# A decoder layer's HGRN2 tail with two token buffers, evictions on ScalarE, and its transfers asked for earlier

## The reference, cut to what matters

```python
def gla_chunked(q, k, v, log_f, s0):
    ...
    def step(S, inp):
        qc, kc, vc, gc = inp
        bcum = jnp.cumsum(gc, axis=1)
        diff = bcum[:, :, None] - bcum[:, None, :]
        dec = jnp.exp(jnp.where(mask, diff, -jnp.inf))
        att = jnp.einsum('blhk,bshk,blshk->blsh', qc, kc, dec)
        o = (jnp.einsum('blsh,bshv->blhv', att, vc)
             + jnp.einsum('blhk,bhkv->blhv', qc * jnp.exp(bcum), S))
        b_last = bcum[:, -1:]
        S = (jnp.exp(b_last[:, 0])[..., None] * S
             + jnp.einsum('bshk,bshv->bhkv', kc * jnp.exp(b_last - bcum), vc))
        return S, o
```

## Time and profile before

| what | value |
|---|---|
| time, median of 3 runs | 1291.14 us (1289.27 to 1294.19) |
| the profiled execution's own time | 1291.79 us |
| its span | 1290.1 us |
| TensorE busy | 1186.7 us, 92% of the span |
| VectorE busy | 605.8 us, 47% |
| ScalarE busy | 445.0 us, 34% |
| mean granted TensorE clock | 0.945 |

### The profile page before, as it was taken

How to read it: one execution, slowest core, us unless ns; L and a number is a source line. 1 busy time by engine, 2 the same in 40 slices (tenths; PEclk the granted TensorE clock), 3 DMA queues, 4 the chain that set the end, 5 groups by cost and what they waited for, 6 DMA issues and landing times.

```text
span 1290.1 us, 25363 instructions
## 1 busy us (share of the span) xinstructions
PE 1186.7 (92%) x10272; PEld 1024.3 (79%) x10272; DVE 605.8 (47%) x1082; ACT 445.0 (34%) x789; POOL 441.2 (34%) x370
## 2 busy tenths in 40 slices
PE   5999999988977769998898899998999999999998
PEld 5999987855654449887797865997999999987775
DVE  4699645236386568512437245257433433421003
ACT  6333243255543123432445134354322322321212
POOL 6443531153406202254251400242344344333331
PEclk9999999989958769898898999998999999999999
DMA  5332321075628730334240676131232322322221
GB/s 143 83 97 67 99 71 52 5 214 179 206 75 276 218 117 4 99 115 117 91 139 20 194 229 196 49 99 44 83 88 86 90 87 86 93 84 82 82 82 69
DMA packets 176381, 139.02 MB, mean 108 GB/s; under 512 B 16007, under 2 KB 162872, under 8 KB 176266
## 3 DMA queue, kind: packets, MB, share of 16 engines
q1 hardware_dynamic: 166610, 115.98, 30.4%
q0 software_dynamic: 7200, 20.23, 5.0%
q10 hardware_dynamic: 2456, 1.21, 0.3%
HBM read 129.41 MB, written 7.97 MB: 106 GB/s over the span
## 4 chain that ended last, share of the span: by engine, by line
PE 71%; DVE 15%; ACT 4%; DMA 3%; issue 3%; POOLq 2%; POOL 2%; SPq 0%; DVEq 0%; ACTq 0%
PE PS L262 64%; PE PS L265 7%; DVE PROJ L1908 3%; DVE SC L681 2%; POOLq L462 2%; DMA W_scratch<-in_cache_moba_v 2%; DVE PROJ L1909 1%; DVE XN L909 1%; DVE XT L681 1%; POOL W_LO L246 1%; DVE PROJ L681 1%; DVE XN_parts L901 1%; DVE XN L681 1%; DMA PROJ<-in_x_sample 1%; ACT W_HI L237 0%
## 5 line engine op out<-in xcount | busy, mean ns | idle before, releaser
L246 POOL TENSOR_TENSOR W_LO<-W,W_HI 128x1024 fp32r<-128x1024 f32 x128 | 314.9, 2465 | 649.3 <-ACT W_HI L237 649.3
L262 PE MATMUL PS<-XN_parts,W_HI 128*128 128x272 f32 x1184 | 340.6, 288 | 0.0
L262 PE MATMUL PS<-OM_parts,W_HI 128*128 128x272 f32 x960 | 277.6, 289 | 0.0
L262 PEld LDWEIGHTS PS<-XN_parts,W_HI 128*128 128x128 f32 x1184 | 223.2, 188 | 0.0
L237 ACT ACTIVATE W_HI<-W 128x1024 fp32r<-128x1024 f32 x128 | 134.2, 1053 | 210.3 <-PE PS L262 210.3
L262 PE MATMUL PS<-OM_parts,W_LO 128*128 128x272 f32 x704 | 203.9, 290 | 0.0
L262 PE MATMUL PS<-SC_parts,W_HI 128*128 128x272 f32 x608 | 180.0, 296 | 4.3 <-POOL W_LO L246 3.1
L262 PEld LDWEIGHTS PS<-OM_parts,W_HI 128*128 128x128 f32 x960 | 181.9, 189 | 0.1
L262 PE MATMUL PS<-SC_parts,W_LO 128*128 128x272 f32 x608 | 176.9, 291 | 0.0
L262 PEld LDWEIGHTS PS<-OM_parts,W_LO 128*128 128x128 f32 x704 | 132.3, 188 | 0.0
L262 PEld LDWEIGHTS PS<-SC_parts,W_HI 128*128 128x128 f32 x608 | 115.7, 190 | 8.4 <-issue 6.3
(11 more groups left out here) (394 smaller groups left out, 2109.7 us busy)
## 6 DMA issues: line engine op xcount, KB each, us to landing
W<-in_w_gu SPq DMA_DIRECT2D x44, 512.0 KB, 3.8
W<-in_w_in SPq DMA_DIRECT2D x30, 512.0 KB, 3.8
W<-in_w_down SPq DMA_DIRECT2D x22, 512.0 KB, 3.7
W_scratch<-in_cache_moba_k SPq DMA_DIRECT2D x64, 128.0 KB, 2.4
W_scratch<-in_cache_moba_k POOLq DMA_DIRECT2D x64, 128.0 KB, 2.5
W_scratch<-in_cache_moba_v SPq DMA_DIRECT2D x64, 128.0 KB, 3.3
W_scratch<-in_cache_moba_v POOLq DMA_DIRECT2D x64, 128.0 KB, 3.5
W<-in_w_xkv SPq DMA_DIRECT2D x16, 512.0 KB, 3.7
```

What stands on the lines that cost most here:

```text
L246: nc.gpsimd.tensor_tensor(hi_lo(n)[1], raw_chunk(n), hi_lo(n)[0].bitcast(F32), ALU.subtract).then_inc(S("weights_split"), 1)
L262: return nc.tensor.matmul(out, lhsT, rhs, start=start, stop=stop, skip_group_check=True)
```

## The change

- HGRN2 gets a tail of its own (`hgrn_tail_tensor`, `hgrn_vector_tail`, `hgrn_tail_scalar`). Token-order keys and values have two buffers for the prompt and one for the samples, token PSUM banks 0 and 1 alternate, outputs use banks 3 and 6, state products 4 and 5. The order of tiles is 0, 1, samples, 2, 3.
- ScalarE makes the token copies (one of 128x512 per tile) and the output copies. The masked values are made by VectorE (4 samples) and ScalarE (4).
- SP asks for the states, decay tiles 0 and 1 and the two rows of log decays between quarters 42 and 44; decay tiles 2, 3 and 4 after its last quarter and level 7. Tiles 0 and 1 are made ready during levels 4 and 5, tiles 2 to 4 in the tail; GDN's first steps no longer make tiles 2 and 3.
- The 17 transposes of the probabilities stand ahead of level 0; each level is then followed by the four quarters that followed the next level before. All 32 value quarters stand ahead of the tail's first transposes.
- GDN's tail is the old code, alone.

```diff
+        def g_decay(i):
+            return g_dec[:, i] if i < 4 else g_dec_s[0:NS]
...
+        h_kv = carve(XN, 1760, 512), carve(XN, 2272, 512), carve(SC, 1120, 512)
...
-            load_pages(sp, [n for n in range(NPG, 64) if issuer(n) == "sync"])
-            after(sp, "ssm")
+            load_pages(sp, [n for n in range(NPG, 44) if issuer(n) == "sync"])
             sp.wait_ge(S("ssm_states_out"), 32)
             sp.dma_start(t_s0, a["state_hgrn"][0].rearrange("b (c e) k v -> (e k) b c v", e=2)).then_inc(S("state_in"), 16)
-            def spread_decays(tile, dst, w, landed="g_spread"):
-                src = decay_rows[:, tile * P:tile * P + w].rearrange("(o h) l -> o h l", o=1)
-                sp.dma_start(dst, src.to_broadcast((w, H, w))).then_inc(S(landed), 16)
+            def spread_decays(i, landed):
+                t0, w, _ = TILES[i]
+                src = decay_rows[:, t0:t0 + w].rearrange("(o h) l -> o h l", o=1)
+                sp.dma_start(g_decay(i), src.to_broadcast((w, H, w))).then_inc(S(landed), 16)
             sp.wait_ge(S("decay_rows_out"), 16)
-            sp.wait_ge(S("h_lv_mm"), H_MM[7])
-            spread_decays(0, g_dec[:, 2], P)
-            spread_decays(1, g_dec[:, 3], P)
-            spread_decays(4, g_dec_s[0:NS], NS)
+            spread_decays(0, "g_spread")
+            spread_decays(1, "g_spread")
             for e in range(2):
                 sp.dma_start(g_logd[e * DH:(e + 1) * DH, :, :],
                              decay_rows.rearrange("(o c e) t -> e o c t", o=1, e=2)[e].to_broadcast((DH, 2, T))).then_inc(S("g_spread"), 16)
+            load_pages(sp, [n for n in range(44, 64) if issuer(n) == "sync"])
+            sp.wait_ge(S("h_lv_mm"), H_MM[7])
+            for i in range(2, NT):
+                spread_decays(i, "g_spread_late")
             after(sp, "hgrn")
-            spread_decays(2, g_dec[:, 0], P, "g_spread2")
-            spread_decays(3, g_dec[:, 1], P, "g_spread3")
...
-        h_vm_ = carve(SC, 2 * T, NB * H * DH)
+        h_vm = carve(PROJ, (C_Z + 4) * T, H, NB, DH)
...
+                if j in (4, 5):
+                    decay_vector(v, j - 4)
...
+        H_TURNS = (0, 1, 4, 2, 3)
+        H_AT = {i: x for x, i in enumerate(H_TURNS)}
+        def h_kv_of(i):
+            return h_kv[i % 2] if i < 4 else h_kv[2][0:NS]
+        def h_turned(i):
+            return bank(H_AT[i] % 2)
+        def h_added(i):
+            return bank(4 + i % 2)[:, 0:2 * DH]
+        def h_out(i):
+            w = TILES[i][1]
+            return bank((3, 6)[H_AT[i] % 2])[:, 0:2 * w]
+        def hgrn_tail_tensor(pe):
+            def turn(i):
+                t0, w, _ = TILES[i]
+                x = H_AT[i]
+                if x >= 2:
+                    pe.wait_ge(S("tail_tok_out"), x - 1)
+                for m_, src in enumerate((h_kd, h_v)):
+                    for k in range(2):
+                        last = tr(h_turned(i)[0:w, 256 * m_ + k * P:256 * m_ + (k + 1) * P], src[:, k, t0:t0 + w], P)
+                last.then_inc(S("tail_tok"), 1)
+            def added(i):
+                kv = h_kv_of(i)
+                pe.wait_ge(S("tail_tok_out"), H_AT[i] + 1)
+                if i >= 2:
+                    pe.wait_ge(S("tail_state"), i - 1)
+                for h in range(H):
+                    last = mm(h_added(i)[h_rows[h], (h // 2) * DH:(h // 2 + 1) * DH], kv[:, h * 64:(h + 1) * 64],
+                              kv[:, 256 + h * 64:256 + (h + 1) * 64], True, True)
+                last.then_inc(S("tail_st"), 1)
+            def output(i):
+                t0, w, _ = TILES[i]
+                kv = h_kv_of(i)
+                if H_AT[i] >= 2:
+                    pe.wait_ge(S("h_o_out"), H_AT[i] - 1)
+                o_ = [h_out(i)[h_rows[h], (h // 2) * w:(h // 2 + 1) * w] for h in range(H)]
+                for h in range(H):
+                    last = mm(o_[h], kv[:, 256 + h * 64:256 + (h + 1) * 64], h_att_of(i, w, h), h < 2, i == 0)
+                if i == 4:
+                    pe.wait_ge(S("state_in"), 32)
+                    for b in range(NB):
+                        own = slice(b * TS, (b + 1) * TS)
+                        for h in range(H):
+                            last = mm(o_[h][:, own], t_s0[h_rows[h], b, h // 2, :],
+                                      h_qe[h_rows[h], h // 2, t0 + b * TS:t0 + (b + 1) * TS], False, True)
+                elif i:
+                    pe.wait_ge(S("tail_state"), i)
+                    for h in range(H):
+                        last = mm(o_[h], t_st[i % 2][h_rows[h], h // 2, :], h_qe[h_rows[h], h // 2, t0:t0 + w], False, True)
+                last.then_inc(S("tail_o"), 1)
+            pe.wait_ge(S("tail_prep"), 1)
+            turn(0)
+            turn(1)
+            yield
+            pe.wait_ge(S("g_beta"), UNITS + 2)
+            added(0)
+            output(0)
+            turn(4)
+            added(1)
+            turn(2)
+            output(1)
+            pe.wait_ge(S("tail_tok_out"), H_AT[4] + 1)
+            output(4)
+            turn(3)
+            yield
+            added(2)
+            output(2)
+            pe.wait_ge(S("tail_vm"), 2)
+            pe.wait_ge(S("tail_root"), 2)
+            for h in range(H):
+                last = mm(bank((2, 7)[h // 2])[h_rows[h], :], h_kv[2][0:NS, h * 64:(h + 1) * 64],
+                          h_vm[0:NS, h].rearrange("p b d -> p (b d)"), True, True)
+            last.then_inc(S("tail_st"), 1)
+            added(3)
+            output(3)
+            yield
+        def h_vm_part(b):
+            return h_vm[0:NS, :, b, :], h_kv[2][0:NS, 256:512].rearrange("p (h d) -> p h d", d=DH), ind[0:NS, b:b + 1]
+            tt(h_kd, hk, h_d, ALU.mult).then_inc(S("tail_prep"), 1)
+            yield
+            def state(i):
+                old, new = t_st[i % 2], t_st[(i + 1) % 2]
+                if i >= 2:
+                    v.wait_ge(S("tail_o"), H_AT[i - 1] + 1)
+                if i:
+                    link(tt(new, old, bc(t_lastp[:, i, :].rearrange("p (c o) -> p c o", o=1), (P, 2, DH)), ALU.mult))
+                v.wait_ge(S("tail_st"), (1, 2, 3, 5)[i])
+                add = h_added(i).rearrange("p (c d) -> p c d", d=DH)
+                last = tt(new, new, add, ALU.add) if i else V.tensor_copy(new, add)
+                last.then_inc(S("tail_state"), 1)
+                v.wait_ge(S("tail_state"), i + 1)
+            state(0)
+            decay_vector(v, 2)
+            state(1)
+            v.wait_ge(S("tail_tok_out"), H_AT[4] + 1)
+            for b in range(NB // 2):
+                dst, src, one = h_vm_part(b)
+                last = V.tensor_scalar(dst, src, one, None, ALU.mult)
+            last.then_inc(S("tail_vm"), 1)
+            decay_vector(v, 3)
+            state(2)
+            yield
+            decay_vector(v, 4)
+            v.wait_ge(S("tail_o"), H_AT[4] + 1)
+            link(tt(t_s0.rearrange("p b c d -> p (b c) d"), t_s0.rearrange("p b c d -> p (b c) d"),
+                    bc(t_lasts.rearrange("p b (c o) -> p (b c) o", o=1), (P, 2 * NB, DH)), ALU.mult))
+            v.wait_ge(S("tail_st"), 4)
+            for c_ in range(2):
+                last = tt(t_s0[:, :, c_, :], t_s0[:, :, c_, :], bank((2, 7)[c_]).rearrange("p (b d) -> p b d", d=DH), ALU.add)
+            last.then_inc(S("states_made"), 1)
+            state(3)
+            V.drain().then_inc(S("fin_made"), 1)
+            v.drain().then_inc(S("tail_state"), 1)
+            yield
+        def hgrn_tail_scalar(s):
+            def kept(i):
+                w = TILES[i][1]
+                x = H_AT[i]
+                if i in (2, 3):
+                    s.wait_ge(S("tail_o"), H_AT[i - 2] + 1)
+                s.wait_ge(S("tail_tok"), x + 1)
+                scopy(h_kv_of(i)[0:w], h_turned(i)[0:w, :]).then_inc(S("tail_tok_out"), 1)
+            def output(i):
+                t0, w, _ = TILES[i]
+                s.wait_ge(S("tail_o"), H_AT[i] + 1)
+                scopy(OM[:, 4:6, t0:t0 + w], h_out(i).rearrange("p (c l) -> p c l", l=w)).then_inc(S("h_o_out"), 1)
+            kept(0)
+            kept(1)
+            yield
+            kept(4)
+            output(0)
+            kept(2)
+            s.wait_ge(S("tail_tok_out"), H_AT[4] + 1)
+            for b in range(NB // 2, NB):
+                dst, src, one = h_vm_part(b)
+                last = A.activation(dst, src, ACT.Copy, scale=one)
+            last.then_inc(S("tail_vm"), 1)
+            output(1)
+            kept(3)
+            decay_scalar(s, 2)
+            yield
+            output(4)
+            output(2)
+            decay_scalar(s, 3)
+            output(3)
+            decay_scalar(s, 4)
+            yield
...
-                if i == 1:
-                    decay_vector(v, 2)
-                    decay_vector(v, 3)
...
-        LANES = "m".join(["pp"] + ["pppp"] * 14 + ["ppp"] * 3 + ["pppp", "p", "", "ppppp"]
```

(3 more changed lines are left out.)

324 lines of the change are left out of this document (148 added, 176 removed).

## The result

The changed kernel takes 1298.05 us (median of 12 runs, 1293.39 to 1307.94) against 1291.14 for the kernel before (12 runs on the same chips). The ratio is 1.0058, with a 95% interval of 1.0033 to 1.0083: slower by 0.6%. My forecast was 1290, the range 1279 to 1303. The time lies in the range, on the other side of no change than the forecast. The profiled execution took 1299.6 us, its span 1298.0.

What follows compares the result with a forecast made beforehand. The prediction took TensorE, busy 92% of the span, as the bound, through its waits and clock. From 1291.79 us, A +4.0, B +4.8, C -8.3 and D -2.2 sum to -1.7, giving 1290; range 1279 to 1303.

Steps and rivals of the forecast that it cites:

- A: Value pages: SP's 32 later reads make TensorE wait about 10 us at quarter 44, 6 come back; +4.0 us.
- My upper end, +9: Upper bound for the value pages: all but one microsecond of the roughly 10 us wait at quarter 44 stays.
- the order of steps: Value pages: transposes one level earlier make levels 0 and 1 some 4 us later, covered by the wait for 37.
- The moved bytes: States, decays and log rows, 1.6 MB (4.6 us of all engines), cost nothing, hidden by SP's 18.6 us of reads.
- B: Between quarter 63 and the tail's first transposes: last level products and keys' product now follow the quarters; +4.8 us, bounds 4.3 to 5.6.
- C: HGRN2 tail: waits for copies go, 19.7 us at clock 0.76 against 28.0; -8.3 us, bounds -12.3 to +0.5.
- Rival 3: HGRN2 tail, dense, at full clock: -12.3 us there, 1286 us in all; chance 0.2.
- D: GDN's start: decay tiles 2 and 3 leave VectorE's work there for the tail; -2.2 us, upper bound -1.5.
- Rival 2: Slower: some 10 us stall at quarter 44 (+9) and a half-clock tail with waits (0); 1303 us, chance 0.2.
- The three parts named for its chance of a clearly faster kernel: Faster by over 6.5 us, chance 0.30: no-stall rival, under half of Rival 3, a tenth of the forecast.
- The list of what to see: Signs expected in the profile after: SP's reads, quarter 44's issue and wait, last quarter, tail length and clock, GDN's start.
- its own last sign: The forecast is wrong as a whole if a stage before 354 or after 484 changes length by over 2 us.

Runs made afterwards that it cites:

- e1: The changed kernel with all 48 of SP's page numbers read ahead of quarter 36 again; 1289.85 us, 0.9991 of the kernel before.
- e2: The kernel before, with SP reading 16 page numbers ahead of quarter 36 and 32 behind quarter 42, no transfer moved; 1299.37 us, ratio 1.0062.
- e3: The changed kernel with 32 of SP's page numbers read ahead of quarter 36 and 16 behind the decays; 1292.06 us, 1.0007 of the kernel before.
- e5: e1 with GpSimd reading 24 of its 48 page numbers ahead of its wait for quarter 35's slot; 1287.68 us, 0.9972 of the kernel before.
- e7: e1 with HGRN2's norm products behind GDN's second tile instead of its first; 1289.66 us, 0.9990 of the kernel before.
- e10: The kernel before with e5's edit alone (24 GpSimd reads ahead of its wait for quarter 35's slot); 1286.55 us, ratio 0.9958.
- e11: e1 with the old order: transposes behind level 0, value quarters one level later, last four behind the tail's first transposes; 1277.79 us, 0.9897 of before.
- e12: e11 with e5's edit (24 GpSimd reads ahead of its wait for quarter 35's slot); 1281.47 us, 0.9913 of the kernel before.
- e4: The kernel before, with both queues reading page numbers for four of their quarters at a time; 1302.5 us, ratio 1.0088.
- e6: e1 with the last four value quarters behind the tail's first two sets of transposes; 1289.91 us, 0.9975 of the kernel before.
- e8: The changed kernel with the edits of e1, e5, e6 and e7 together; 1285.76 us, 0.9956 of the kernel before.
- e9: e8 with SP's first 40 page numbers read between key quarters 24 to 32 and log decays sent behind quarter 36; 1294.5 us, 1.0019 of before.

## Why the prediction was wrong, step by step

- **A, +4.0: this step failed; it was +15.0.** The stall itself was forecast (quarter 44 out at 415, a wait of about 10 us; measured 418.96 and 12.09). What failed is "Of 10 us I let 6 come back out of the 8.2 us of idle time": nothing came back. I read TensorE's idle time in the window of 395.7 to 442.4 as slack. In the trace of before it is made of waits for the very stream that was held up; of TensorE's waits from 395.7 on, this line has them:

```profile
PE PS L262 <- DMA W_scratch<-in_cache_moba_v: 11.4, 7, 4.4
```

  The longest, 4.4 us, is the one for 37 that ends as the window begins; the other 7.0 are 85% of the 8.2 idle. From the use of quarter 44 to the end of 63 the kernels before, after, e1, e2, e3, e5, e7, e10, e11 and e12 take 33.3, 34.4, 35.9, 34.9, 35.9, 32.8, 33.4, 33.3, 34.6 and 34.1 us, wherever they start (e4 has a gap of its own in it and takes 46.2; in e6, e8 and e9 TensorE comes to the last four quarters only after the tail's first transposes). My upper end, +9, came from the same error.
- **What sets that pace** is in part argued. From 409.1 to 442.4 the DMA share is 0.95 in the kernel before, so its engines had little left. In the changed kernel it is 0.91 from 423 to 450 but 0.64 from 450 on, where TensorE waits 3.81 us for quarter 63. There GpSimd's queue is late: quarters 61 and 63 are not among the numbers read ahead, and it reads four for each, 2.26 us, before it sends them. Quarter 57's first transfer and quarter 63, after:

```profile
434.62 0.55 POOL L487 DMA_DIRECT2D W_scratch<-in_cache_moba_v  x1 [0.26 <-issue]
...
448.99 2.29 POOL L487 DMA_DIRECT2D W_scratch<-in_cache_moba_v  x4 [2.26 <-issue]
```

  From the first of these to the end of the second it takes 16.7 us, and 16.7 in e1, e10 and e11 and 17.3 in the kernel before. No run moved these last reads.
- **A, the order of steps: a cost put at nothing.** The later levels were "covered by the same wait for 37", and that held: 37 is used at 395.25, before at 395.73. What I did not price is that levels stand behind page waits in TensorE's list, so that one of them is left over at the end. By the median this is the larger loss: e1 to e11, 12.1 us (with the open part of the clock in it), against 8.2 for the reads (after to e1). In place, at the tail's first transposes, which come 27.0 us later than before, net: 9.5 go with the reads, 10.1 with the order, and 7.5 are left in e11. e6 shows that moving back the last four quarters alone does not help; whether the transposes' place or the quarters' place carries it was not tried apart.
- **The moved bytes.** I costed them at nothing, because the 18.6 us of reads covered them. That was nearly so in the changed kernel (quarter 39 is used at 400.18 instead of 398.26, and the wait for 44 swallows it), and only there: without the reads quarter 44 is 4.4 us later (e11 beside before) and 7.7 (e12 beside e10), about the 4.6 us and more that the prediction worked out for the bytes. The rule of the Trainium skill ("Trainium Kernel Development and Optimization", Key Constraints), that all issuers share the same 16 DMA engines, is the one that counts once the reads are gone; the DMA share of 1.08 above agrees with it. How much of this is bytes and how much SP's time to send them was not tried apart.
- **B, +4.8:** 457.4 to 462.7 is 5.3, inside its bounds, at clock 0.50.
- **C, -8.3:** 19.7 forecast from the first transposes to GDN, 20.0 measured, at clock 0.67 instead of 0.76 and with 0.7 us of waits instead of 2.9; two errors that cancel. Rival 3's number was within reach: in e11 the four last quarters and the tail take 18.6 us at clock 0.91.
- **D, -2.2: +0.4.** The decay products had stood where VectorE now waits. VectorE's timeline after, in their place:

```profile
489.89 3.68 DVE L686 TENSOR_TENSOR PROJ<-SC,PS 64x256 f32<-64x256 f32 x8 [2.40 <-PE PS L262]
```

  It waits 2.40 us for the third tile's products, which stand behind 4.1 us of norm products at half clock (484.77 and 486.75 above). Where these run at full clock (e11, 1.18 and 1.08), the stretch is 11.17 us and the forecast's 11.05 is nearly met. So D hung on the clock, of which the forecast took no account here.
- **The sum and the rivals.** With these four terms as measured the sum is +12.7 in place of -1.7. By it the time would have been 1304.5, just outside my range. That the measured 1298.05 lies inside it is luck: behind GDN's start the profiled pair differs by 5.0 us the other way, and nothing ties that to the change. Rival 2 names what happened at quarter 44. Its A, +9, was too low and its C, 0, too high, since the tail held. The three parts named for its chance of a clearly faster kernel add up to 0.285 at most, not 0.30.
- **The list of what to see.** The 32 reads in one piece (17.7 us for 18 to 19), B's stretch and C's (20.0) came as written, and there was no wait for the token copies (0.7 us idle in the whole tail). Quarter 44 went out later than written (418.96 for 413 to 417; SP came to the states at 394.28 instead of 391), and the wait was longer (12.09 for 7 to 11). C's clock (0.67 for 0.7 to 0.8), "the last use of a value quarter at 444 to 449" and D's 2 us did not come. By its own last sign the forecast is wrong as a whole: behind 484 the profiled pair differs by 5 us, though that cannot be told from what executions differ by.

The account of the medians: before to e11 is -13 us (by its interval -9 to -18), e11 to e1 +12, the order of steps and what goes with it, e1 to after +8, the 32 reads; together +7. So the new tail with what else e11 keeps of the change helps, and two edits beside it cost more.
